# Token shift from the PSUM bank, and a reordered schedule of the RWKV-7 stage, in a one-core transformer kernel

## What is computed

```python
def rwkv7_time_mix(z, mu, ...):
    z = z + (token_shift(z) - z) * mu          # token_shift: the row of the token before, 0 for the first
    r, k, v, xw, xa, xg = jnp.split(z, RWKV_SPLITS, axis=-1)
    logw = -jax.nn.softplus(-(w0 + jnp.tanh(xw) @ w2)) - 0.5
    decay = jnp.exp(-jnp.exp(logw))
    a = jax.nn.sigmoid(a0 + xa @ a2)
    g = jax.nn.sigmoid(xg) @ g2
    kk = heads(k * k_k);  kk = kk / max(norm(kk), 1e-12)
    k = k * (1.0 + (a - 1.0) * k_a)
    def step(state, inp):                       # 8 heads of 64, over 256 tokens
        sa = einsum('bhvk,bhk->bhv', state, a_t)
        state = state * w_t + sa * b_t + v_t * k_t
        y = einsum('bhvk,bhk->bhv', state, r_t)
    ...                                         # group norm of y, bonus (r.k) v, times g
```

## Time and profile before

| | |
|---|---|
| median of 3 runs | 1102.18 us (1101.38 to 1103.61) |
| profiled execution | 1101.91 us, its span 1100.1 us |
| TensorE matmul / weight load busy | 999.6 us (91%) / 961.7 us (87%) |
| VectorE / ScalarE busy | 674.8 us (61%) / 507.7 us (46%) |
| mean granted TensorE clock | 0.94 |
| DMA | 172.35 MB, 157 GB/s mean |
| chain that ended last | PE 49%, DVE 6%, ACT 4%, issue 3% of the span; the line L2262 alone 36% |

### The profile page before, as it was taken

One profiled execution on the slowest core, in us unless ns is written; L12 is line 12 of the kernel. 1 busy time (PEld: TensorE's weight loads), 2 busy tenths in 40 slices (PEclk: granted clock), 3 DMA queues, 4 the chain that ended last, 5 costly groups with the idle time before them and its releaser, 6 DMA issues.

```text
span 1100.1 us, 19713 instructions
## 1 busy us (share of the span) xinstructions
PE 999.6 (91%) x8709; PEld 961.7 (87%) x8709; DVE 674.8 (61%) x846; ACT 507.7 (46%) x583; POOL 5.6 (1%) x12
## 2 busy tenths in 40 slices
PE   5679997998999999899879879998988899999986
PEld 4679997998999998898879878978978899999985
DVE  3588889765555456864587745324566566466465
ACT  2043552444553578544553332235755555354342
POOL 2000000000000000000000000000000000000000
PEclk8579998999999999999879999979999999999998
DMA  8779646873562443866233222123331456555521
GB/s 293 251 232 308 205 154 207 255 231 123 184 192 90 141 133 98 259 225 212 77 102 124 84 77 79 40 77 114 123 118 61 151 188 219 179 181 194 174 73 39
DMA packets 165584, 172.35 MB, mean 157 GB/s; under 512 B 3984, under 2 KB 162124, under 8 KB 165372
## 3 DMA queue, kind: packets, MB, share of 16 engines
q1 hardware_dynamic: 162380, 164.41, 46.8%
q10 hardware_dynamic: 3120, 6.69, 1.7%
HBM read 170.03 MB, written 1.05 MB: 156 GB/s over the span
## 4 chain that ended last, share of the span: by engine, by line
PE 49%; DVE 6%; ACT 4%; issue 3%; DVEq 0%; ACTq 0%
PE pj L2262 36%; ACT w_hi L803 1%; DVE w_lo L1221 1%; PE m_all L1993 1%; PE m_all L1995 1%; PE m_all L1982 1%; PE pj L2221 1%; PE pj L2222 1%; PE pj L2223 1%; PE m_all L1767 1%; DVE work L1421 1%; PE pj L2082 1%; PE m_all L2116 1%; PE m_all L1922 0%; PE m_all L2061 0%
## 5 line engine op out<-in xcount | busy, mean ns | idle before, releaser
L1221 DVE TENSOR_TENSOR w_lo<-raw,w_hi 128x2048 fp32r<-128x2048 f32 (+1 forms) x135 | 303.5, 2253 | 165.0 <-ACT w_hi L803 164.6
L2262 PE MATMUL pj<-h_hi,w_hi 128*128 128x256 f32 x1232 | 357.5, 290 | 26.5 <-issue 8.0
L2262 PE MATMUL pj<-h_lo,w_hi 128*128 128x256 f32 x1232 | 351.4, 285 | 0.0
L2262 PE MATMUL pj<-h_hi,w_lo 128*128 128x256 f32 x1232 | 350.8, 285 | 0.0
L803 ACT ACTIVATE w_hi<-raw 128x2048 fp32r<-128x2048 f32 (+1 forms) x135 | 253.1, 1878 | 117.5 <-PE pj L2262 51.8
L2262 PEld LDWEIGHTS pj<-h_hi,w_hi 128*128 128x128 f32 x1232 | 237.2, 193 | 33.2 <-issue 22.5
L2262 PEld LDWEIGHTS pj<-h_lo,w_hi 128*128 128x128 f32 x1232 | 237.6, 193 | 0.3
L2262 PEld LDWEIGHTS pj<-h_hi,w_lo 128*128 128x128 f32 x1232 | 237.3, 193 | 0.2
L2262 PE MATMUL pj<-y_hi,w_hi 128*128 128x256 f32 x600 | 169.2, 282 | 3.5 <-DVE y_lo L1680 1.9
L2262 PE MATMUL pj<-y_hi,w_lo 128*128 128x256 f32 x600 | 168.3, 280 | 0.0
L2262 PE MATMUL pj<-y_lo,w_hi 128*128 128x256 f32 x600 | 168.2, 280 | 0.0
(11 more groups left out here) (332 smaller groups left out, 1209.3 us busy)
## 6 DMA issues: line engine op xcount, KB each, us to landing
raw<-in_odd_in_w_dram SPq DMA_DIRECT2D x28, 1024.0 KB, 5.3
raw<-in_ada_w_dram SPq DMA_DIRECT2D x24, 1024.0 KB, 5.9
raw<-in_w_in_dram SPq DMA_DIRECT2D x23, 1024.0 KB, 5.3
raw<-in_even_in_w_dram SPq DMA_DIRECT2D x20, 1024.0 KB, 5.2
raw<-in_w_ff_in_dram SPq DMA_DIRECT2D x16, 1024.0 KB, 5.4
raw<-in_w_ff_out_dram SPq DMA_DIRECT2D x16, 1024.0 KB, 5.2
raw<-in_even_out_w_dram SPq DMA_DIRECT2D x8, 1024.0 KB, 5.9
raw<-in_odd_out_w_dram SPq DMA_DIRECT2D x8, 1024.0 KB, 5.3
```

Of the source, the lines that this page charges most:

```text
L1221: V.tensor_tensor(w_lo[:, i % SPL, 0:n], raw[:, u % RAW, 0:n], w_hi[:, i % SPL, 0:n].bitcast(F32), ALU.subtract).then_inc(S(f"split{i % SP ...
L2262: m = nc.tensor.matmul(to, a_, b_, start=(s == 0 and q == 0 and (fb == 0 or not together)), stop=(s == len(steps_) - 1 and q == 2), skip_g ...
```

## The change

- **Token shift.** z + (shifted - z) mu is computed as (1 - mu) z + mu shifted. ScalarE evacuates a bank as a scaled copy (Identity, scale column `one_less_mu`), one for each of a job's two blocks of 256 columns, straight into the destination; the padded buffers and their four memsets go. VectorE adds mu times the bank, shifted by one column (255 columns, one multiply-add for each block), and only then is the bank free. This is done per job, not per name; `key_sq` is cut in two halves, each behind its own. `one_less_mu` (14 columns) is made in `ada_first`.
- **Splits.** "behind" and two of the "late" marks go, so that w_hi and w_lo are made two units ahead of the projection throughout, except at wv 1.
- **Order.** rw_cross and rw_blocks stand between wr 0 and wr 1; every rw_u and rw_t is followed by a new attention projection or wr/side work, ahead of the evacuations; the shifts of wv 0, wv 1, wr 0 and wr 1 move behind key_unit, behind wr 1 and into the first half level; vt, bkt, bonus and mats each move about one half level later.
- **Solve.** `solve_u` does its 8 products of 64x64 first, then its 8 of 128x64; `solve_y` of chunk 1 does its 16 products of 128x64 first, then the 8 of 64x64, and start is set for b = 0 only.
- **Norm.** The Square of gn_var becomes a step `gn_sq` ahead of the job wga 2 and ahead of the table switch.

```diff
     step("mix_pre")
     second("wx", "wx", 3840, 0, n=160, blocks=(64, 96))
-    step("shift_x")
+    step("shift", ("wx", 0))
     attn = [("aq", "rope", 0, i, "F") for i in range(3)] + [("ak", "rope", 768, i, "F") for i in range(3)]
     attn += [("av", "copy_t", 1536, i, "T") for i in range(3)]
     waiting = []
@@ -282,7 +282,6 @@
         name, kind, c0, i, lay = attn.pop(0)
         second(name, kind, c0, i, lay)
         early(name, i)
-        jobs[name, i]["behind"] = 1
         waiting.append((name, i))
 
     def side(name, i):
@@ -302,80 +301,79 @@
         schedule.append(("split_" + part, (name, i)))
 
     second("wk", "shifted", 2816, 0)
+    step("shift", ("wk", 0))
+    step("key_sq", 0)
     second("wk", "shifted", 2816, 1)
-    late("wk", 1)
-    split("hi", "wk", 1)
     step("lora_w")
     step("lora_a")
-    step("shift_k")
-    step("key_sq")
-    split("lo", "wk", 1)
+    step("shift", ("wk", 1))
+    step("key_sq", 1)
     step("decays")
     second("wv", "shifted", 3328, 0)
-    late("wv", 0)
     step("decay_exp")
     step("key_norms")
     step("decay_rest")
     step("key_kt")
-    split("hi", "wv", 0)
     second("wv", "shifted", 3328, 1)
     late("wv", 1)
     step("key_unit")
-    split("lo", "wv", 0)
     split("hi", "wv", 1)
     split("lo", "wv", 1)
-    for i in range(2):
-        second("wr", "shifted", 2304, i)
+    step("shift", ("wv", 0))
+    second("wr", "shifted", 2304, 0)
     step("rw_cross")
     step("rw_blocks", 0)
     step("rw_blocks", 1)
-    ahead()
-    step("shift_r")
+    second("wr", "shifted", 2304, 1)
+    step("shift", ("wv", 1))
 
     def during(m, part):
 
         if (m, part) == (0, "u"):
+            for i in range(2):
+                step("shift", ("wr", i))
+            step("rw_inputs")
             ahead()
-            step("rw_inputs")
         elif (m, part) == (0, "t"):
             ahead()
             catch_up()
-            step("shift_v")
         elif (m, part) == (1, "u"):
+            ahead()
+            catch_up()
+            step("rk")
+        elif (m, part) == (1, "t"):
+            ahead()
             catch_up()
             side("vt", 0)
             side("vt", 1)
+        elif (m, part) == (2, "u"):
             ahead()
-            step("rk")
-        elif (m, part) == (1, "t"):
             catch_up(3)
             side("bkt", 0)
             side("bkt", 1)
+        elif (m, part) == (2, "t"):
             ahead()
-        elif (m, part) == (2, "u"):
             catch_up(3)
             side("bonus", 0)
             side("bonus", 1)
+        elif (m, part) == (3, "u"):
             ahead()
-        elif (m, part) == (2, "t"):
             catch_up(3)
             for n in range(2):
                 side("mats", n)
-            catch_up()
+        elif (m, part) == (3, "t"):
+            ahead()
+            catch_up(3)
             for n in range(2, 4):
                 side("mats", n)
-        elif (m, part) == (3, "u"):
-            catch_up(4)
-            ahead()
-        elif (m, part) == (3, "t"):
+        elif (m, part) == (4, "u"):
+            catch_up(3)
             for n in range(4, 6):
                 side("mats", n)
-            catch_up(3)
-        elif (m, part) == (4, "u"):
+        elif (m, part) == (4, "t"):
+            catch_up(2)
             ahead()
-        elif (m, part) == (4, "t"):
-            ahead()
-            catch_up(2)
+            catch_up()
 
     for m in range(LEVELS):
         for part in ("u", "t"):
@@ -407,6 +405,7 @@
     step("gn_mean")
     finish("wga", 0)
     finish("wga", 1)
+    step("gn_sq")
...
-                        split_to(last_unit[what] + SPL - jobs[what].get("behind", 0))
+                        split_to(last_unit[what] + SPL)
...
+            def gn_sq():
+                act.wait_ge(S("gn_c"), 1)
+                nc.scalar.activation(flat(S_["gsum"], 4), flat(S_["y"], 4), ACT.Square).then_inc(S("gn_sq"), 1)
+
             def gn_var():
                 act.preload_act_table_set(LOG_EXP)
-                act.wait_ge(S("gn_c"), 1)
-                nc.scalar.activation(flat(S_["gsum"], 4), flat(S_["y"], 4), ACT.Square).then_inc(S("gn_sq"), 1)
...
                     projected(act, key)
-                    act.wait_ge(S("zpad"), 4)
-                    z = zpad(key[0])
-                    if kind == "wx":
-                        link(nc.scalar.activation(z[0:64, 0, 1:], b[0:64, 0:T], ACT.Copy))
-                        done_reading(nc.scalar.activation(z[0:96, 1, 1:], b[0:96, T:2 * T], ACT.Copy), key)
-                    else:
-                        done_reading(nc.scalar.activation(z[:, 2 * i:2 * i + 2, 1:], two, ACT.Copy), key)
+                    for rows_, fb, to, _, keep in shift_parts(*key):
+                        nc.scalar.activation(to, b[rows_, fb * T:(fb + 1) * T], ACT.Identity, bias=small_zero[rows_], scale=keep).then_inc(S(f"kept_{key[0]}"), 1)
...
+        def shift_parts(name, i):
+
+            at, mu = shifted[name]
+            for fb in range(2):
+                n = (64, 96)[fb] if name == "wx" else P
+                b = 2 * i + fb
+                yield slice(0, n), fb, flat(at + b, 1)[0:n, :], vec("rwkv_mu_2", mu + b)[0:n], one_less_mu[0:n, mu + b:mu + b + 1]
...
+                link(V.tensor_scalar(one_less_mu, vec("rwkv_mu_2", 0, 14), -1.0, 1.0, ALU.mult, ALU.add))
...
+            def shift(key):
+                dve.wait_ge(S(f"kept_{key[0]}"), 2 * key[1] + 2)
+                b = bank_of(key)
+                for rows_, fb, to, mu, _ in shift_parts(*key):
+                    i_ = V.scalar_tensor_tensor(out=to[:, 1:], in0=b[rows_, fb * T:(fb + 1) * T - 1], scalar=mu, in1=to[:, 1:], op0=ALU.mult, op1=ALU.add)
+                    if fb == 0:
+                        link(i_)
+                done_reading(i_, key)
+                evacuated(dve, key)
...
                 lower, upper_ = tiles
                 for h in range(RW_H):
                     nc.tensor.matmul(M[2][lower, hcol(h)], tt_of(c)[lower, h, :], wu[lower, hcol(h)], start=True, stop=True)
+                for h in range(RW_H):
                     m = nc.tensor.matmul(M[2][upper_, hcol(h)], um_of(c)[:, h, :], wu[:, hcol(h)], start=True, stop=True)
                 m.then_inc(S("rw_u0"), 1)
...
                     to = M[3][hs, b * P:(b + 1) * P]
-                    nc.tensor.matmul(to, wu[:, hcol(h)], br[:, h, :], start=True, stop=False, skip_group_check=True)
+                    nc.tensor.matmul(to, wu[:, hcol(h)], br[:, h, :], start=(b == 0), stop=False, skip_group_check=True)
                     m = nc.tensor.matmul(to, vt[:, c, hd], ka[:, h, P:2 * P], start=False, stop=(c == 0), skip_group_check=True)
-                    if c == 1:
-                        m = nc.tensor.matmul(to, s0[hs, b, :], ar_[hs, b, c, 1, :], start=False, stop=True, skip_group_check=True)
+                if c == 1:
+                    for h, b, half, hs in heads:
+                        m = nc.tensor.matmul(M[3][hs, b * P:(b + 1) * P], s0[hs, b, :], ar_[hs, b, c, 1, :], start=False, stop=True, skip_group_check=True)
                 m.then_inc(S("rw_y"), 1)
```

More of the change, by code:

```diff
@@ L603, in program @@
         sv_tok = flat(O_["svv"], 8).rearrange("p (n d) -> p n d", n=2)
+        one_less_mu = small[:, 46:60]
         small_zero = small[:, 40:41]
@@ L1080, in ple_x @@
                     nc.scalar.activation(h_hi[:, k, :], x[:, k, :], ACT.Copy).then_inc(S("operand_hi"), 1)
-            steps = dict(mix_pre=mix_pre, shift_x=shift_x, lora_w=lora_w, lora_a=lora_a, decay_exp=decay_exp, decay_rest=decay_rest, key_sq=key_sq, key_norms=key_norms, rw_cross=rw_cross, rw_join=rw_join, rw_joined=rw_joined, solve_w=solve_w, solve_u=solve_u, solve_y=solve_y,
-                         gn_mean=gn_mean, gn_var=gn_var, at_s=at_s, at_t=at_t, at_o=at_o, mixed=mixed, ffn_pre=ffn_pre,
+            steps = dict(mix_pre=mix_pre, shift=shift, lora_w=lora_w, lora_a=lora_a, decay_exp=decay_exp, decay_rest=decay_rest, key_sq=key_sq, key_norms=key_norms, rw_cross=rw_cross, rw_join=rw_join, rw_joined=rw_joined, solve_w=solve_w, solve_u=solve_u, solve_y=solve_y,
+                         gn_mean=gn_mean, gn_sq=gn_sq, gn_var=gn_var, at_s=at_s, at_t=at_t, at_o=at_o, mixed=mixed, ffn_pre=ffn_pre,
                          turn_p=turn_p, split_p=split_p, ple_x=ple_x, ple_post=ple_post, load_x=load_x, first_sum=first_sum, params=params, norm=norm, final_norm=final_norm, sgu_v=sgu_v, windows=windows, gla_z=gla_z, gla_decay=gla_decay, gla_kt=gla_kt, gla_o=gla_o, gla_n=gla_n, sb_z=sb_z, sb_c=sb_c, sb_o=sb_o)
@@ L1286, in final_norm @@
                 projected(dve, ("oo", 3))
-                for name in ("wr", "wk", "wv", "wx"):
-                    V.memset(zpad(name)[:, :, 0:1], 0.0).then_inc(S("zpad"), 1)
                 dve.wait_ge(S("rstd"), 3)
@@ L1935, in run_vt @@
                 bank_free(key)
-                pe.wait_ge(S("shift"), 4)
+                for i in range(2):
+                    evacuated(pe, ("wv", i))
```

56 lines of the change are left out of this document (16 added, 40 removed).

## The result

The changed kernel takes 1056.35 us (median of 4 runs, 1055.42 to 1058.64), the kernel before 1101.78 on the same chip (4 runs, 1101.10 to 1103.61): ratio 0.9588, 95% interval 0.9569 to 0.9608, 45 us less. The forecast was 1059.0, with a range of 1053 to 1075. The profiled execution took 1056.31 us, with a span of 1054.5 where it was 1100.1.

What follows compares the result with a forecast made beforehand. TensorE was taken to bound the kernel, with 27.3 of 149.8 us lost to holes and slowed matmuls. 25.4 + 4.1 + 9.6 + 1.1 + 3.1 - 0.2 = 43.1 us off 1101.9 gave 1059, range 1053 to 1075.

Steps and rivals of the forecast that it cites:

- stage A: holes, slowed pieces, new waits: First lora product to solve_w: 27.3 us of holes and slowed matmuls, less 0.9 new waits and 1 for hand-offs: 25.4.
- solve_u, both: Solve: with products grouped by tile kind, each solve_u falls from 4.1 to 2.05 us, saving 4.1 together.
- solve_y 1: The second solve_y: with grouped products it takes 2.8 us instead of 12.4, saving 9.6.
- wga 1 at full clock: Projection behind the solve: it took 6.9 to 7.0 us at clock 0.82; full clock saves 1.1.
- the Square: Norm: moving ScalarE's Square ahead of wga 2 removes the 3.1 us wait before gn_var.
- seven slowed pieces: TensorE matmuls between 571.02 and 662.4 us running slower than at full clock, about 7.3 us in all.
- the 1 us taken off for hand-offs: Lora products to solve_w: an allowance for missed hand-offs, lowering the gain from 26.4 to 25.4 us.
- Rival (e): Splits stay late, held by ScalarE's queue order; only the solve and norm gain: 1084 us, chance 0.02.
- for k it counts more: Token shift for k: behind wk 1, 1.0 + 0.75 us of VectorE work remain instead of 5.0.
- Rival (b): Solve: the clock, not the tile kind, was slow in solve_y; grouped products stay at 1.2 GHz: 1063 to 1067, chance 0.15.
- Rival (c): Solve: loads and products on one tile do not overlap, each solve_u takes 11.3 us: 1077.5, chance 0.03.
- Rival (a): Levels: VectorE hands over 1.2 us late at each of ten half levels, costing 12 us: 1071, chance 0.17.

Runs made afterwards that it cites:

- a_blocks: The changed kernel with rw_cross and rw_blocks behind wr 1 again, as before the change: 1064.65 us, ratio 0.9647 to the kernel before.
- a_late: The changed kernel with wk 1's and wv 0's splits late again and the attention projections' splits one unit less ahead: 1063.73 us, ratio 0.9636.
- a_during: The changed kernel with the five levels in their old order, and aq 0 and wr's shift ahead of rw_u 0: 1070.14 us, ratio 0.9699.
- a_shift: The changed kernel's order and splits with the old token shift (padded buffers, plain copies, a subtraction and four multiply-adds per name): 1056.75 us, ratio 0.9571.
- a_u: The changed kernel with solve_u alternating its 64x64 and 128x64 products again: 1066.70 us, ratio 0.9668 to the kernel before.
- a_y: The changed kernel with chunk 1's third solve_y product inside the head loop again, and the start flag for b = 1 back: 1058.79 us, ratio 0.9598.

## Why the prediction was right

**The sum.** 43.1 us were forecast off the profiled execution, and 45.6 came. By steps:

| step | forecast | measured |
|---|---|---|
| stage A: holes, slowed pieces, new waits | 25.4 | 28.3 |
| solve_u, both | 4.1 | 3.8 |
| solve_y 1 | 9.6 | 9.4 |
| wga 1 at full clock | 1.1 | 1.0 |
| the Square | 3.1 | 3.1 |
| one_less_mu | -0.2 | below what shows |
| ahead of stage A and behind B | 0 | -0.3 (1.0 won, 1.3 lost) |

The measured steps come to 45.3; the missing 0.3 is for the most part gn_var's sums (1.7 us instead of 2.0). Stage A is off by 2.9 us, and its rows say where. I had listed seven slowed pieces with 7.3 us (against their lengths in the changed kernel they come to 7.6); TensorE's busy time fell by 8.8, so 1.5 were missed (the chain shows only the long pieces). Idle time of 0.9 us was to be left, and 0.5 was, which makes 0.4. And the 1 us taken off for hand-offs that I might have missed was not needed. The 8.8 us can be read only with the trace of after in hand; with them the forecast would have been 1057.5. All that was to be seen is there: no hole ahead of wr 0, its w_lo at 556.2, solve_u at 2.1 to 2.2, solve_y 1 at 3.0 and clock 1.00, no wait for the Square.

**The order.** Right in size and cause, and a_blocks, a_late and a_during show it part by part. One cause was half seen: the 7.7 us were laid to VectorE's queue alone, and ScalarE's w_hi was late as well. The change cured both, so the forecast did not suffer. Rival (e) fell with them.

**The token shift.** The durations were right (a pair of multiply-adds in 1.0 us) but one was too high: a pair of ScalarE's scaled copies takes 1.02 us where 1.4 was counted. The step's worth was not: a_shift gives it 0.5 us, which can't be told from nothing. The prediction gave it no term of its own, and said "for k it counts more"; it hardly counts.

**The solve.** The terms were right, their assignment was wrong. I gave 9.6 us to the grouping of solve_y 1 and 4.1 to that of solve_u. Undone alone they cost 4.5 and 9.8: much of solve_y's 12.4 us was a clock that the alternating solve_u brings down. The sum of the two came out because both groupings went in together, and that is luck as far as the mechanism goes: with one of them alone the forecast would have been some 6 us off. Rival (b) took the clock for a cause of its own, which would stay; in fact it went with the alternation.

Rival (c) is refuted: it made 11.3 us of a grouped solve_u, and 2.1 to 2.2 were measured. Loads do overlap running products of the same tile. 16 records of 222 ns and their 16 loads of 133 to 138 ns took 1.15 us in the rows above, 0.07 us a record, and from 674.1 to 676.2 the loads were busy for 1.98 us and the products for 2.10. The Trainium skill's sentence that a load passes a running matmul only where the row group differs (TensorE: Matmul & The Clock Gate, "The mechanism" in Part 3) is not what these rows show; the same section also lets a load pass that goes to the background weight buffer, and that they do not contradict. Another of its pages names a cost that the grouping would save: changing the tiling mode drains the TensorE (TensorEngine Tiling (Array Packing), "Key Properties"). The traces fit it and price the alternation, though they don't show that a drain is the reason: 14 changes fewer in a solve_u save 1.9 us, 0.14 each; 14 fewer in solve_y 1 save 4.5 (with the start flag), 0.32 each.

**Rival (a)** did not come, though its place and its price were real: 12.9 us more of VectorE work cost 1.8 in stage A, 25.2 cost 14.5, and in the profiled execution 7.7 more behind it. My 78% of load was the right number to look at (79% measured), and the margin to the bound about 11 us.

## What to carry to other kernels

A hole that a profile puts down to "issue" ahead of a projection is worth following into the queue of the engine that makes its operand: the split was not slow, it stood behind other work. Look at the queues of all engines that make it: here w_hi was late on one and w_lo on the other. Count a hole with the slowed matmuls behind it, and expect more of them than the chain lists (7.3 us listed here, 8.8 measured). Place filler behind every hand-off before making the hand-off cheaper: the order of the levels was worth 14.7 us, the cheaper token shift 0.5. Small products on tiles of different kinds gained here by being grouped by kind, for their own time (3.8 us in solve_u) and for that of what comes after them (some 6). When two edits touch neighbouring products, undo each alone: their sum can be right and their shares wrong.

## What was not expected of the hardware

- TensorE, busy without a break, lost clock during alternating 64x64 and 128x64 products: 1.00 in the 8.0 us before and 0.83 in solve_u 0, then whole again, 0.91 in the second solve_u and 0.51 in solve_y 1 (a_u). In the kernel before both solve_u kept 1.00 and the fall came in solve_y 1 (0.55). With solve_u grouped it kept 1.00, even through an alternating solve_y 1 of 7.5 us (a_y).
- Behind the same lora products, with the same instructions up to there, the clock was 0.71 or 0.72 in five executions and 1.00 in four.
- A ScalarE copy with a scale column and a bias column from PSUM, 128x256, has a record of 0.56 us, and two in a row take 1.02, where one from SBUF with an fp32r result has a record of 0.60.
